# Stages without barriers, and attention probabilities turned by transposes, in a fused four-layer kernel

## The reference

```python
# first block: layer 0 even, layer 1 odd
h = h + 0.5 * swiglu(rms_norm(h, ffn1_g), wg, wu, wd)
h = h + (even_mixer if layer % 2 == 0 else odd_mixer)(rms_norm(h, mix_g), ...)
h = h + 0.5 * swiglu(rms_norm(h, ffn2_g), ...)
h = h + sigmoid(rms_norm(h, ple_g) @ ple_wgate) * (p @ ple_wproj)
# second block
y = concat([pool_mixer(za), retention(rq, rk, rv), mem_attention(xq, mem_n)]) * silu(gate)   # even
y = concat([nsa_attention(...), mem_attention(xq, mem_n)]) * silu(gate)                      # odd
h = h + y @ w_out
# every attention, one query block of 128 rows and one head at a time:
prob = softmax(q @ k.T * scale + bias_or_mask);  out += gate * prob @ v
```

## Time and profile before

| | |
|---|---|
| median of three runs | 3636.24 us (3629.88 to 3636.94) |
| the profiled execution | 3634.45 us, its span 3632.5 us |
| TensorE busy | 3266.0 us, 90% |
| weight loads (PEld) | 2593.9 us, 71% |
| GpSimd, VectorE, ScalarE busy | 1204.4, 1200.8, 1124.2 us |
| mean granted TensorE clock | 0.936 of full speed |

### The profile page before, as it was taken

One profiled execution on the slowest core, in us unless ns is written; L12 is line 12 of the kernel. 1 busy time (PEld: TensorE's weight loads), 2 busy tenths in 40 slices (PEclk: granted clock), 3 DMA queues, 4 the chain that ended last, 5 costly groups with the idle time before them and its releaser, 6 DMA issues. The chain is left out here.

```text
span 3632.5 us, 37332 instructions
## 1 busy us (share of the span) xinstructions
PE 3266.0 (90%) x14634; PEld 2593.9 (71%) x14634; DVE 1200.8 (33%) x2313; ACT 1124.2 (31%) x1954; POOL 1204.4 (33%) x530
## 2 busy tenths in 40 slices
PE   7999988989999899998379999778889889999998
PEld 5888666657888678886258888565747767777776
DVE  3001566741011520117941011534243222145342
ACT  3222323332222322223032223342222332355422
POOL 4444331023444344444124444332314433210043
PEclk9999999799999899999689999889989989989999
DMA  3333211012333223333013333222212225200022
GB/s 124 99 97 95 78 59 30 1 41 93 96 96 97 66 81 99 93 99 96 29 52 88 98 93 98 76 81 67 85 35 87 76 73 184 92 30 1 12 87 76
DMA packets 76242, 277.95 MB, mean 77 GB/s; under 512 B 8439, under 2 KB 9335, under 8 KB 75428
## 3 DMA queue, kind: packets, MB, share of 16 engines
q1 hardware_dynamic: 76068, 275.57, 24.4%
HBM read 273.39 MB, written 2.15 MB: 76 GB/s over the span
## 5 line engine op out<-in xcount | busy, mean ns | idle before, releaser
L418 POOL TENSOR_TENSOR w_lo<-ring,w_hi 128x1024 fp32r<-128x1024 f32 x473 | 1142.5, 2417 | 2349.3 <-ACT w_hi L398 2349.2
L433 PE MATMUL ps<-x_hi,w_hi 128*128 128x512 f32 x2408 | 953.9, 396 | 89.7 <-DVE x_lo L582 77.8
L434 PE MATMUL ps<-x_lo,w_hi 128*128 128x512 f32 x2408 | 941.1, 391 | 0.0
L435 PE MATMUL ps<-x_hi,w_lo 128*128 128x512 f32 x2408 | 941.0, 391 | 0.0
L398 ACT CAST w_hi<-ring 128x1024 fp32r<-128x1024 f32 x473 | 494.5, 1047 | 1032.6 <-PE ps L435 1027.1
L433 PEld LDWEIGHTS ps<-x_hi,w_hi 128*128 128x128 f32 x2408 | 460.7, 191 | 197.0 <-issue 103.7
L434 PEld LDWEIGHTS ps<-x_lo,w_hi 128*128 128x128 f32 x2408 | 460.9, 191 | 96.4 <-issue 4.3
L435 PEld LDWEIGHTS ps<-x_hi,w_lo 128*128 128x128 f32 x2408 | 459.6, 191 | 94.7
L433 PE MATMUL ps<-r_hi,w_hi 128*128 128x512 f32 x1120 | 441.7, 394 | 53.1 <-DVE r_lo L845 47.1
L434 PE MATMUL ps<-r_lo,w_hi 128*128 128x512 f32 x1120 | 440.0, 393 | 0.0
L435 PE MATMUL ps<-r_hi,w_lo 128*128 128x512 f32 x1120 | 439.8, 393 | 0.0
(11 more groups left out here) (181 smaller groups left out, 2704.3 us busy)
## 6 DMA issues: line engine op xcount, KB each, us to landing
ring<-in_stream SPq DMA_DIRECT2D x473, 512.0 KB, 3.6
arena<-in_cmp_w SPq DMA_DIRECT2D x16, 512.0 KB, 4.5
arena<-frev SPq DMA_DIRECT2D x1, 5376.0 KB, 18.5
h<-in_x SPq DMA_DIRECT2D x1, 2048.0 KB, 8.1
arena<-in_mem SPq DMA_DIRECT2D x2, 1024.0 KB
out<-arena SPq DMA_DIRECT2D x4, 512.0 KB
arena<-in_p SPq DMA_DIRECT2D x2, 512.0 KB
arena<-in_pool_recip SPq DMA_DIRECT2D x1, 1024.0 KB
```

What stands on the lines that cost most here:

```text
L418: self.nc.gpsimd.tensor_tensor(self.w_lo[:, n % SPLIT, :], self.ring[:, n % RING, :], self.w_hi[:, n % SPLIT, :].bitcast(F32), ALU.subtrac ...
L433: nc.tensor.matmul(out, a[0], b[0], start=start, stop=False)
L434: nc.tensor.matmul(out, a[0], b[1], start=False, stop=False)
L435: return nc.tensor.matmul(out, a[1], b[0], start=False, stop=stop)
```

## The change

**Stages.** `Stage` takes the place of `nc.Block`: it calls each engine's function in turn and adds nothing, so the engines run from one stage into the next. What the barrier kept in order is now kept by tokens (a semaphore and the value that it must reach): `bank_read` holds, for each of PSUM's eight banks, the token of its last reader, and TensorE waits for it on the bank's first use in a stage; `inverted` is raised after a reciprocal; `after`, `tables`, `loaded` name other data; `early_after` holds SyncE's early loads until their target in SBUF is free. SyncE no longer waits for its early loads at the end of a stage. The lams stage is gone: its product and exponential are in `start`.

**Attention.** VectorE scales the probabilities in place over all w columns, and TensorE turns them by `transpose` against the identity. The wait of VectorE for the turn three units back (`diag` ring of three) goes with the diagonals.

```diff
+class Stage:
+    def __init__(self, nc):
+        self.sync, self.gpsimd = (lambda f: f(nc.sync)), (lambda f: f(nc.gpsimd))
+        self.scalar, self.tensor, self.vector = (lambda f: f(nc.scalar)), (lambda f: f(nc.tensor)), (lambda f: f(nc.vector))
...
+    def bank(self, pe, b):
+        if self.bank_read[b]:
+            pe.wait_ge(*self.bank_read[b])
...
+        for token in self.early_after:
+            sp.wait_ge(*token)
         for dst, src in self.early:
             sp.dma_start(dst, src).then_inc(self.aux.handle, 16)
...
-        if self.early:
-            sp.wait_ge(self.aux.handle, self.aux.at(0))
...
 # MeanSquare
         act.wait_ge(self.summed.handle, self.summed.at(KT // 2))
+        if self.inverted.base:
+            act.wait_ge(*self.inverted.token())
...
-        self.k.nc.vector.reciprocal(self.inv, self.root[:, 0:self.n])
+        self.k.nc.vector.reciprocal(self.inv, self.root[:, 0:self.n]).then_inc(self.inverted.handle, 1)
+        dve.wait_ge(*self.inverted.token(1))
...
 # every stage, as dense_f
-    with nc.Block() as block:
+    with Stage(nc) as block:
...
                 if m >= 8:
                     pe.wait_ge(read.handle, read.at(m - 7))
+                else:
+                    k.bank(pe, m)
...
+    tokens = [read.token(m + 1) for m in range(slabs)]
+    for m in range(slabs):
+        k.bank_read[m % 8] = tokens[m]
...
 # attention
-                pe.wait_ge(diag.handle, diag.at(i + 1))
+                pe.wait_ge(weighted.handle, weighted.at(i + 1))
...
-                    ins = nc.tensor.matmul(k.ps[0:rows, 4 + i % 2, j * P:(j + 1) * P],
-                                           ex[:, i % 5, j * P:j * P + rows], dg[:, i % 3, :], start=True, stop=True)
+                    ins = nc.tensor.transpose(k.ps[0:rows, 4 + i % 2, j * P:(j + 1) * P],
+                                              ex[:, i % 5, j * P:j * P + rows], k.c("ident"))
...
-                if i >= 3:
-                    dve.wait_ge(turned.handle, turned.at(i - 2))
+                p = ex[:, i % 5, 0:u.w]
                 if u.gate is None:
-                    ins = nc.vector.tensor_scalar(dg[:, i % 3, :], k.c("ident"), inv[:, i % 5:i % 5 + 1], None, ALU.mult)
+                    ins = nc.vector.tensor_scalar(p, p, inv[:, i % 5:i % 5 + 1], None, ALU.mult)
                 else:
-                    ins = nc.vector.tensor_scalar(dg[:, i % 3, :], k.c("ident"), inv[:, i % 5:i % 5 + 1], u.gate,
-                                                  ALU.mult, ALU.mult)
+                    ins = nc.vector.tensor_scalar(p, p, inv[:, i % 5:i % 5 + 1], u.gate, ALU.mult, ALU.mult)
...
 # mem_attention
+    with Stage(nc) as block:
+        block.scalar(lambda act: act.wait_ge(*loaded))
         MeanSquare(k, mem, NMEM, inv).alone(block)
+    if early:
+        k.early, k.early_after = early, [k.s["inverted"].token()]
```

More of the change, by code:

```diff
@@ L482, in _ @@
                                  stop=True).then_inc(product.handle, 1)
+            pe.wait_ge(dots.handle, dots.at(1))
+            nc.tensor.matmul(k.ps[:, 3, 0:2], k.c("ones"), small[:, 0:2], start=True, stop=True).then_inc(product.handle, 1)
         @block.vector
@@ L489, in _ @@
             square.dve(dve)
+            dve.wait_ge(lam_exp.handle, lam_exp.at(1))
+            k.vlink(nc.vector.tensor_tensor(small[:, 4:5], small[:, 3:4], small[:, 2:3], ALU.subtract))
+            k.vlink(nc.vector.tensor_scalar(small[:, 5:6], small[:, 4:5], -0.2, None, ALU.add))
+    for b in (1, 2):
+        k.bank_read[b] = copied.token(b)
+    k.bank_read[3] = lam_exp.token(1)
     x_in.advance(16)
@@ L723, in dense_t @@
             block.vector(meanwhile)
+    tokens = [read.token(u + 1) for u in range(tts * len(widths))]
+    for u, token in enumerate(tokens):
+        k.bank_read[u % 8] = token
     part.advance(parts[-1])
@@ L789, in dense_gated @@
         norm.close()
+    for m in range(n):
+        if not square or m % 8 != square.bank:
+            k.bank_read[m % 8] = gate.token(m + 1)
     for g in (done, gate) + (() if square else (read,)):
@@ L857, in dve, with alone @@
         self.los.advance(self.n)
-    def alone(self):
+    def alone(self, tile_ready=None):
         k = self.k
-        with k.nc.Block() as block:
+        with Stage(k.nc) as block:
             @block.sync
@@ L979, in __init__, with attention @@
         self.w = key.shape[-1]
-def attention(k, units, scratch, background=()):
+def attention(k, units, scratch, background=(), after=()):
     nc, s = k.nc, k.s
@@ L1029, in values @@
                 ins.then_inc(summed.handle, 1)
+            for token in after:
+                pe.wait_ge(*token)
             for i in range(n + 4):
@@ L1155, in act, with dense_rope @@
             self.k.nc.scalar.activation(dst, dst, ACT.Sin)
-def dense_rope(k, stage, jobs, rot, cos, sin, scratch, norm=None):
+def dense_rope(k, stage, jobs, rot, cos, sin, scratch, norm=None, tables=None):
     nc, s = k.nc, k.s
@@ L1274, in dense_rope @@
         norm.close()
+    for m in range(max(0, n - 4), n):
+        k.bank_read[m % 4] = read.token(m + 1)
+    for m in range(n - 2, n):
+        k.bank_read[6 + m % 2] = used.token(m + 1)
+    for a in range(max(0, len(rank) - 2), len(rank)):
+        k.bank_read[4 + a % 2] = rooted.token(a + 1)
     for g in (squared, sums, rooted, normed):
@@ L1304, in _ @@
         def _(act):
+            for token in after:
+                act.wait_ge(*token)
             for i in range(1, TT):
@@ L1673, in odd_mixer, with mem_attention @@
     rows_add(k, "od_out", o, [P] * KT, 1.0).alone()
-def mem_attention(k, layer, out, base):
+def mem_attention(k, layer, out, base, loaded, early=None):
     nc = k.nc
@@ L1742, in pool_windows, with pool_mixer @@
     return windows
-def pool_mixer(k, za, out, wg):
-    nc, done = k.nc, k.s["product_done"]
-    with nc.Block() as block:
+def pool_mixer(k, za, out, wg, after):
+    nc, done, copied = k.nc, k.s["product_done"], k.s["pool_copied"]
+    with Stage(nc) as block:
         @block.tensor
         def _(pe):
+            for token in after:
+                pe.wait_ge(*token)
             for m, g, f0, f1, lo, hi, over in POOL_PRODUCTS:
+                if lo == 0:
+                    k.bank(pe, m)
                 for i, (c, k0, k1) in enumerate(over):
@@ L1913, in _ @@
                     for m in range(2):
+                        if u % 8 == 0 and li == 0:
+                            k.bank(pe, 2 * kind + m)
                         ins = nc.tensor.matmul(k.ps[:, 2 * kind + m, 0:m2], w1[u % 2][:, li, m * P:(m + 1) * P],
@@ L2039, in second_odd @@
                                   last=(b == 1), dst=qh))
-    attention(k, units, scr)
+    attention(k, units, scr, after=values[-1:])
     gate_and_project(k, 1, y, [P] * 16, scr)
```

253 lines of the change are left out of this document (173 added, 80 removed).

## The result

The changed kernel takes 3536.43 us (median of 4 runs, 3535.36 to 3537.73) against 3636.59 for the kernel before on the same chip: a ratio of 0.9729, 95% interval 0.9712 to 0.9745. That is 100 us less; forecast were 138 less (3498), with a range of 3465 to 3585.

A forecast was written before the change was run, and what follows sets the result against it. TensorE, busy for 3266.0 of 3632.5 us, was taken as the bound. Barriers 96.2, clock 12, NSA 20, memory attentions 6 and first attention 4 sum to 138 us saved: 3498 us, range 3465 to 3585.

The forecast's parts named there:

- 12 for the clock: Clock behind closed gaps: about five wholly removed gaps give back 2.4 us more each, 12 us, bounds 0 and 20.
- (c): Stages starting with a normalisation, TensorE waiting behind VectorE L582 (77.8 us in 12): removing barriers saves 22.5 us.
- four starts with an old inverse: ple_g and xq, twice each: only GpSimd's split held the barrier before VectorE's first multiplication; 3.7 us saved each, 14.8.
- the entry of the first attention: VectorE's first bias add can start at 573.75, not after two barriers and lams near 579: 5 us.
- The mean of squares: Mean of squares of the memory, twice: squares no longer wait for reciprocal and barrier, 4 us each, 8.
- so I keep 4: First attention, shorter turns of 160 blocks: 18 us, of which 4 kept because VectorE is busy and engines are chained.
- NSA: 20: NSA attention: 288 shorter turns save 32 us, less 12 for some 28 us more at clock 0.50.
- rival D: Low clock in NSA's narrow half and the rest of the first attention: about 3580 us, from 3540; chance 0.18.
- Rival B: Attention: the transpose takes two passes as the matmul did, no turn gain, no lower clock: 3528 us; chance 0.15.
- C: Attention: the transpose takes a quarter, more gain in NSA and memory attention, better first attention: 3475 us; chance 0.12.
- Rival E: Clock stays at 0.50 in all of NSA and in the first attention under transposes: 3653 us; chance 0.08.
- rival A: The forecast itself, barriers and attention together: 3498 us, its own range 3470 to 3520; chance 0.47.

## Why the prediction was right, and where it was not

**The barriers**: 96.2 us of gaps and 12 for the clock were forecast, 108 in all. The seams gave 92.4 in the profile, and the kernel without barriers and with the old turn is 100.3 us below the kernel before. Near as that is, it is two errors that partly cancel: in that kernel TensorE's idle time fell by 77.0 us, not 96, and the same instructions took 22.8 us less, not 12 (matmuls' ends are modelled, so the division is rough).

The gaps were sized too high, most plainly in (c). Of its 22.5 us, 14.8 were four starts with an old inverse at 3.7 each. They gave 1.6, 1.7, 1.9 and 2.3, 7.4 together. The overlap shown with the result names the step: VectorE's work now runs beside GpSimd's split and takes longer. The whole wait for the low half fell by 11.6 us. The 2.4 us of clock behind each closed gap were my estimate from the start of ple_p: 12 products took 5.2 us at 0.50 there, and 36 took 8.5 at 1.00, so that 22 would fit into 5.2 and 10 of them are worth 2.4. No run shows that a closed gap gives them back, and none shows the 12 us; where it was tested, at gate0, it failed: the clock was 0.50 over its start with the gap and without it. If the 22.8 us are all the clock's, it gave more than the 12 in total; which gaps they came from was not measured.

By parts: gate0 8.0 forecast, and its lead grew by 9.0; rv (one of L1174) 5.5 and 5.8; ple_p 1.5 each and 1.44 each; the entry of the first attention 5 and 2.7, as TensorE's lead did not help VectorE's chain of index_scores, which is the late one there (10.2 us of waiting at L1089 for the first scaling). The mean of squares gave about 6 of 8 us. Where VectorE was the bound, nothing came (the mixing: 61.7 us of waiting before, 63.2 now), as forecast.

**The turn**: the size of a transpose was right (0.111 forecast, 0.108 found), VectorE's price too (70 ns forecast for each 128 columns, 67 found). What failed is the step from there to the time, "so I keep 4" for the first attention and "NSA: 20". The first attention lost 11.5 us, NSA gave 10.8, all attentions together 3.7 of the forecast 30, and the two kernels that differ in the turn alone (3535.64 and 3536.43) show none of it. Two causes are shown. One is the clock: rival D was at work, with its price in the other place, since the low stretch grew by 68 us in the first attention and 20 in NSA. I had put it at 28 us in NSA and none in the first attention, though that attention had the longest low stretch in the trace before. At the forecast's own 0.43 us for each, the 68 are 29 us against the 18 that the shorter turns save there: an estimate that comes near the 11.5 lost. The other is a wait that no rival named: the values now came to ScalarE's copy before it was done, and of the 0.57, 0.80 and 1.03 us that a period at full clock should lose, 0.23, 0.34 and 0.54 were left. Over twelve heads the missing part is some 15 us. With 9 for the clock (20 at 0.43) it leaves 8 of the forecast 32 in NSA, by estimate; 10.8 were found.

Rival B (two passes, 0.222 us) and C (a quarter, 0.057) are out by the trace, with 0.108 found. Rival E had the sign right for half of the change, since the turn alone makes the kernel slower (ratio 1.0015), but not by its mechanism: the clock did not stay at 0.50 in all of NSA, where it was 0.87 on average.

Of the signs, the waits on PEq are gone, a transpose takes 0.11 us, and the low stretch of NSA is 51 us, as forecast (24 + 28), though it was 31 and not 24 before. TensorE's idle time is 301, not near 270, and L629's waits are 66, not 55. That the total fell into the range is in part luck: 3536 lies outside rival A's own 3470 to 3520, and a range that also had to hold B and D caught it.

## What to carry to other kernels

A barrier between stages cost here what the slowest engine still had to do: TensorE stood for 4.38 us at the end of xq, behind a split, and for 8.03 ahead of gate0, behind the norm. Most of the price could be read from TensorE's gaps one by one: the part of them that would go was put at 96.2 us, and without the barriers its idle time fell by 77.0 and the total by 100.3. What waited for a data chain of another engine only moved (61.7 us at the mixing before, 63.2 now), and VectorE, which the barrier had kept apart from GpSimd's split, took 3.50 us beside it for two multiplications where it had taken 1.41. Work taken from TensorE in a stage that waits on other engines need not be a gain: with the shorter turns the granted clock of the first attention was 0.62 where it was 0.80 with the old ones, and the attention took 172.2 us and not 160.6. So look at the low stretches first, and measure the edit by itself. When one step of a pipeline between engines gets shorter, look at what the next engine does first in its round: ScalarE's copy ahead of its exponential gave 36.6 us with the short turn, and with the old one 2 us that are within the intervals.

## What the runs showed of the hardware

Issuing a useless second transpose made the kernel faster (3536.43 to 3515.69 us where it was done selectively): the granted clock of the first attention was 0.62 with single transposes, and 0.79 and 0.88 in the profiles of two kernels with double ones. In the narrow units of NSA attention a period is 3.95 us at 0.50 with single transposes for all twelve, and 2.83 at 1.00 with double ones. A transpose of 128 by 128 in fp32 took 0.108 us from start to start at full clock and came as one instruction with one weight load, where the fp32 matmul came as two. In the two kernels with double ones, alike up to the end of the first attention, the clock there was 0.50 for 67 us in one profile (to 579.5, and 640.9 to 695.6) and for 36 in the other (to 580.3, and 658.8 to 682.8), and the attention took 8.7 us less in the second. A VectorE multiplication or subtraction of 128 by 512 that ran beside GpSimd's split took 1.9 to 2.8 us instead of about 0.7.
